# Layer norms of a two-block fp32 transformer kernel: mean read from PSUM, column sums over five tiles of squares, two output blocks on ScalarE

## The reference

```
h = concat(meta, x)
first_block:  even mixer (differential and forgetting attention) -> LN -> squared-ReLU MLP -> LN
              retention -> LN -> squared-ReLU MLP -> LN
second_block: SwiGLU -> LN(ln1); HGRN2 + spatial gating -> LN(ln2);
              cross attention to LN(mem) -> LN(ln3); SwiGLU -> LN(ln4)
LN(x) = (x - mean(x)) * rsqrt(mean((x - mean(x))^2) + 1e-5) * g + b
```

## Time and profile before

| | |
|---|---|
| time, median of 3 runs | 2793.22 us (2792.32 to 2794.8) |
| time of the profiled execution | 2793.86 us |
| span of the profiled execution | 2792.1 us |
| PE busy | 2707.3 us, 97% |
| DVE busy | 1281.0 us, 46% |
| ACT busy | 1016.3 us, 36% |
| POOL busy | 283.2 us, 10% |
| mean granted TensorE clock | 0.987 of full |

### The profile page before, as it was taken

One profiled execution on the slowest core, in us unless ns is written; L12 is line 12 of the kernel. 1 busy time (PEld: TensorE's weight loads), 2 busy tenths in 40 slices (PEclk: granted clock), 3 DMA queues, 4 the chain that ended last, 5 costly groups with the idle time before them and its releaser, 6 DMA issues.

```text
span 2792.1 us, 39535 instructions
## 1 busy us (share of the span) xinstructions
PE 2707.3 (97%) x16362; PEld 2360.0 (85%) x16362; DVE 1281.0 (46%) x2178; ACT 1016.3 (36%) x1630; POOL 283.2 (10%) x357
## 2 busy tenths in 40 slices
PE   8999999999999999999999999999999999999997
PEld 7888899999988888788888888888888887888886
DVE  5544654334532323563334543435657655633333
ACT  4554443222322223352223432323567443522221
POOL 0000300001200000210000310002211121200003
PEclk9999999999999999999999999999999999999998
DMA  3111233222111212232222132222321212232220
GB/s 139 54 47 47 83 123 107 91 91 77 46 61 63 97 61 76 91 106 91 98 98 91 70 118 98 91 84 68 121 76 66 93 46 99 82 101 97 95 64 31
DMA packets 66531, 232.94 MB, mean 83 GB/s; under 512 B 8880, under 2 KB 9264, under 8 KB 65968
## 3 DMA queue, kind: packets, MB, share of 16 engines
q1 hardware_dynamic: 66352, 230.41, 24.8%
HBM read 228.25 MB, written 2.10 MB: 83 GB/s over the span
## 4 chain that ended last, share of the span: by engine, by line
PE 86%; DVE 5%; ACT 4%; POOL 2%; issue 2%; DMA 1%; SPq 0%; DVEq 0%; POOLq 0%; ACTq 0%
PE ps L578 75%; PE ps L887 2%; POOL R L2624 2%; PE ps L1013 1%; PE ps L588 1%; DVE R L1890 1%; PE ps L767 1%; PE ps L727 1%; DVE HT L1884 1%; ACT HT L1240 1%; POOL S L2610 1%; PE ps L874 1%; PE ps L598 1%; PE ps L1110 1%; PE ps L611 1%
## 5 line engine op out<-in xcount | busy, mean ns | idle before, releaser
L578 PE MATMUL ps<-XH,WH 128*128 128x264 f32 (+2 forms) x1856 | 538.3, 332 | 14.4 <-DVE XL L2584 8.6
L578 PE MATMUL ps<-XH,LENT 128*128 128x512 f32 (+2 forms) x2096 | 532.1, 343 | 8.0 <-DVE XL L1906 7.9
L578 PE MATMUL ps<-XL,WH 128*128 128x264 f32 (+2 forms) x1856 | 523.6, 324 | 0.0
L578 PE MATMUL ps<-XH,WL 128*128 128x264 f32 (+2 forms) x1856 | 522.7, 324 | 0.0
L578 PE MATMUL ps<-HH,LENT 128*128 128x264 f32 (+2 forms) x2220 | 491.1, 319 | 1.9 <-DVE LENT L1862 1.9
L1862 DVE TENSOR_TENSOR WL<-RAW,WH 128x1024 fp32r<-128x1024 f32 (+1 forms) x232 | 286.5, 1235 | 270.9 <-ACT WH L1210 270.6
L578 PEld LDWEIGHTS ps<-XH,LENT 128*128 128x128 f32 x2096 | 359.1, 190 | 60.0 <-DVE XL L1906 11.8
L578 PEld LDWEIGHTS ps<-HH,LENT 128*128 128x128 f32 x2220 | 361.4, 190 | 32.0 <-DVE LENT L1862 2.3
L578 PEld LDWEIGHTS ps<-XH,WH 128*128 128x128 f32 x1856 | 319.1, 189 | 56.7 <-issue 19.1
L578 PEld LDWEIGHTS ps<-XH,WL 128*128 128x128 f32 x1856 | 318.9, 189 | 28.1
L578 PEld LDWEIGHTS ps<-XL,WH 128*128 128x128 f32 x1856 | 319.1, 189 | 26.6
(11 more groups left out here) (215 smaller groups left out, 2625.1 us busy)
## 6 DMA issues: line engine op xcount, KB each, us to landing
RAW<-in_wf SPq DMA_DIRECT2D x128, 512.0 KB, 3.3
RAW<-in_wr SPq DMA_DIRECT2D x48, 512.0 KB, 3.3
RAW<-in_wg SPq DMA_DIRECT2D x44, 512.0 KB, 3.3
RAW<-in_wu SPq DMA_DIRECT2D x44, 512.0 KB, 3.3
RAW<-in_wd SPq DMA_DIRECT2D x32, 512.0 KB, 3.3
RAW<-in_we SPq DMA_DIRECT2D x24, 512.0 KB, 3.3
RAW<-in_wm SPq DMA_DIRECT2D x24, 512.0 KB, 3.3
RAW<-in_wro SPq DMA_DIRECT2D x16, 512.0 KB, 3.3
```

Source lines behind the costliest of these rows:

```text
L578: mm = e.matmul(o[:, to:to + m], wt, xt[:, k, c0 + a * m:c0 + (a + 1) * m], start=(n == 0 and j == 0), stop=(n == nk - 1 and j == 2))
```

## The change

- The total is multiplied by a matrix `PART` of 1/1024 instead of `ONE`, so PSUM holds the mean. VectorE subtracts it from there. ScalarE's copy of the mean (L1231) and the signal `mean` are gone; the bank is given back after the last subtraction.
- VectorE adds only square 3 to square 1. `stat` takes five tiles: `HT` slots 2 (squares 1 and 3), 6 (square 5), 1 (squares 0, 2, 4), 3 (square 6), 4 (square 7).
- Blocks 2 and 5 of `r_out` are written by ScalarE (`r_act`), behind the `XH` of the same block, in all norms but `mem`.
- ScalarE's wait for the previous half's `r_out` stays, but now stands before the table load and the squares only.
- At attention's end, 3 of the 7 steps of `ends[1]` stay ahead of `even_back(41)`, 2 stand between its transposes and the value product, 2 behind the value product.
- In the ends of `ln10`, `quiet` is set from the third end on.

```diff
@@ tensor, layer_norm
         def layer_norm(ln, half, T, sums, mark, pump, first):
             pump(first)
-            o = bank(("total", ln, half), 1, (S.mean, ln, half))
+            o = bank(("total", ln, half), 1, (S.centre, ln, half, 7))
             w.wait_ge(*mark)
-            e.matmul(o[:, 0:T], ONE[:, :], sums, start=True, stop=True).then_inc(*S.total(ln, half))
+            w.wait_ge(*S.const["one"])
+            e.matmul(o[:, 0:T], PART[:, :], sums, start=True, stop=True).then_inc(*S.total(ln, half))
             pump(17)
-            rstd((ln, half), [(HT[:, 1, 0:T], S.add_pool[(ln, half, 4)]), (HT[:, 2, 0:T], S.add_dve[(ln, half, 7)])],
+            rstd((ln, half), [(HT[:, 2, 0:T], S.add_dve[(ln, half, 3)]), (HT[:, 6, 0:T], S.sq[(ln, half, 5)]),
+                              (HT[:, 1, 0:T], S.add_pool[(ln, half, 4)]), (HT[:, 3, 0:T], S.sq[(ln, half, 6)]),
+                              (HT[:, 4, 0:T], S.sq[(ln, half, 7)])],
                  T, (S.normed, ln, half, 7), pump, 3)
@@ all three, even_back
             if i == 4:
-                pump(1)
+                pump(1 if t < 7 else 2)
@@ all three, even
             even_back(40, pump)
-            for k in range(7):
-                next(ends[1])
+            pump = pumping(ends[1])
+            pump(3)
             even_back(41, pump)
+            pump(2)
@@ scalar, layer_norm
             w.wait_ge(*S.total[ln, half])
             if normed[0]:
                 w.wait_ge(*S.r_out[normed[0]])
-            e.activation(HT[:, 0, 0:T], acc(("total", ln, half), 1)[:, 0:T], ACT.Copy, scale=inv).then_inc(*S.mean(ln, half))
+                if normed[0][0] != "mem":
+                    w.wait_ge(*S.r_act[(*normed[0][:2], ACT_OUT[-1])])
...
+                if ln != "mem" and k in ACT_OUT:
+                    w.wait_ge(*S.normed[ln, half, k])
+                    e.activation(res(k), HT[:, T_SLOT[k], 0:T], ACT.Identity, bias=pcol(ln + "b", k),
+                                 scale=pcol(ln + "g", k)).then_inc(*S.r_act(ln, half, k))
                 pump(3)
@@ scalar and vector, down_norm
-            for nm, idx in ENDS[ln]:
+            for n, (nm, idx) in enumerate(ENDS[ln]):
+                ah.quiet = ln == "ln10" and n > 1
@@ vector, layer_norm
             pump(first)
+            mean = acc(("total", ln, half), 1)[:, 0:T]
             for k in range(8):
-                w.wait_ge(*S.mean[ln, half])
+                w.wait_ge(*S.total[ln, half])
                 w.wait_ge(*ready(k))
-                e.tensor_tensor(res(k), res(k), HT[:, 0, 0:T], ALU.subtract).then_inc(*S.centre(ln, half, k))
-                if k in (4, 6):
-                    add_square(k - 1)
+                e.tensor_tensor(res(k), res(k), mean, ALU.subtract).then_inc(*S.centre(ln, half, k))
+                if k == 4:
+                    w.wait_ge(*S.sq[ln, half, 3])
+                    e.tensor_tensor(HT[:, 2, 0:T], HT[:, 2, 0:T], HT[:, SQ_SLOT[3], 0:T],
+                                    ALU.add).then_inc(*S.add_dve(ln, half, 3))
                 pump(1)
-            add_square(6)
-            add_square(7)
```

More of the change, by code:

```diff
@@ L286, in build_program @@
     ID = sb("ID", [P, P])
-    ONE = sb("ONE", [P, P])
+    ONE, PART = sb("ONE", [P, P]), sb("PART", [P, P])
     SM = sb("SM", [P, 256])
@@ L525, in first_steps, with out_mark @@
         return (6, 16 if ln == "ln1" else 8)[half]
+    ACT_OUT = (2, 5)
+    def out_mark(ln, half, k):
+        return (S.r_act if ln != "mem" and k in ACT_OUT else S.r_out), (ln, half, k)
     def sums_at(name, idx, half):
@@ L1904, in lower @@
                 w.wait_ge(*S.x_hi[ln, half, k])
-                w.wait_ge(*S.r_out[ln, half, k])
+                sig, event = out_mark(ln, half, k)
+                w.wait_ge(*sig[event])
                 e.tensor_tensor(XL[:, k, c:c + T], res(k), XH[:, k, c:c + T].bitcast(F32),
@@ L1921, in layer_norm @@
                 for k in range(8):
-                    r_mark[k][half] = (S.r_out, (ln, half, k))
+                    r_mark[k][half] = out_mark(ln, half, k)
         def residual(name, idx, m, c, T, half, alpha):
@@ L2622, in layer_norm @@
             for k in range(8):
-                w.wait_ge(*S.normed[ln, half, k])
-                e.tensor_scalar(res(k), HT[:, T_SLOT[k], 0:T], pcol(ln + "g", k), pcol(ln + "b", k), ALU.mult,
-                                ALU.add).then_inc(*S.r_out(ln, half, k))
+                if out_mark(ln, half, k)[0] is S.r_out:
+                    w.wait_ge(*S.normed[ln, half, k])
+                    e.tensor_scalar(res(k), HT[:, T_SLOT[k], 0:T], pcol(ln + "g", k), pcol(ln + "b", k), ALU.mult,
+                                    ALU.add).then_inc(*S.r_out(ln, half, k))
                 for m in between.get(k, ()):
@@ L2646, in down_norm @@
                 layer_norm(ln, half, T // 2, lambda k: R[:, k, c:c + T // 2], dst, {} if half else between)
+        e.memset(PART[:, :], 1.0 / 1024).then_inc(*S.const("part"))
         e.memset(ONE[:, :], 1.0).then_inc(*S.const("one"))
@@ L2756, in sync @@
             for half in (0, 1):
-                w.wait_ge(*S.r_out["ln4", half, k])
+                sig, event = out_mark("ln4", half, k)
+                w.wait_ge(*sig[event])
             e.dma_start(out[:, k, :], R[:, k, NM:TW]).then_inc(*S.out_done(k))
```

10 lines of the change are left out of this document (2 added, 8 removed).

## The result

The changed kernel takes **2802.35 us** (median of 7 runs, 2799.74 to 2808.92) against 2793.22 (7 runs of the kernel before beside it, 2792.32 to 2794.8). The ratio is 1.0032, with a 95% interval of 1.0023 to 1.0042: slower by 9 us. The forecast was 2791.6; its own case ended at 2798 and the widest range named at 2800. The profiled execution is the longest of the seven (2808.92 us, span 2807.1), so its granted clock of 0.984 overstates the loss.

The account below looks back on a forecast made before the run. TensorE, busy 97% of the span, was taken as the bound. Terms +2.4 - 2.4 - 2.0 - 1.0 + 1.4 = -1.6 us gave 2792.3 from the profiled 2793.86, or 2791.6 us as median; range 2786 to 2798.

Parts of the forecast that it names:

- The second part of the norm: Output blocks 2 and 5 on ScalarE: `XL` waits in six first halves fall, -2.0 us, bounds -5 to +3.
- Waits that go at the statistics: TensorE's waits in the norms' statistics go outside ln4's last half, restarts included: 19.8 us removed.
- three leads: Norm statistics: square taken directly, mean's copy gone, two adds fewer; with four tiles' time, over 3 us of lead.
- the slow add: VectorE's add before the statistics in ln4's last half; the first tile was expected ready behind it about 2776.5.
- Work that comes: Three more tiles of one-column matmuls per norm half on TensorE: 22.2 us added, net +2.4 with the waits removed.
- Attention's end: Moved steps cover the waits at value product and eighth steps: -2.4 us, bounds 0 and -2.8.
- `quiet`: In ln10's ends nothing is left to hold back from the third end on; TensorE's 2.91 us wait stays: 0.
- The last half of ln4: At the kernel's end, squares begin earlier and five tiles end near 2780.9: -1.0 us, between 0 and -3.
- The clock: Low-clock stretches behind the norms' statistics: one more of 3.41 us than now, +1.4 us.
- the edge between 2.19 and 2.27 us: Norm halves whose statistics and wait took 2.27 us or more lost clock; those of 2.19 or less did not.
- the clock falls in every half: Rival: eight spared norm halves also fall to the low clock, +11 in place of +1.4, 2801 us; chance 0.13.
- The clock recovers: Rival: seven 256-column norm halves stay at full clock, three of 264 fall, -9.4 us, 2781 us; chance 0.16.

Follow-up runs that it names:

- a_noact: The changed kernel with all eight output blocks written by GpSimd, none by ScalarE; 2792.42 us, ratio 0.9993.
- b_mean: The kernel before with the mean read from PSUM (ScalarE's copy gone) as the only change; 2776.86 us, ratio 0.9938.
- a_two_noact: The changed kernel with two tiles of squares and all output blocks on GpSimd; mean from PSUM and moved attention steps stay; 2776.65 us, ratio 0.9934.
- a_twice: a_two_noact with each statistic's tiles run through a second time, the attention's statistics included; 2806.29 us, ratio 1.0046.
- a_one: The changed kernel with one tile and GpSimd's output blocks, but five tiles and ScalarE's blocks in ln4's second half; 2781.52 us, ratio 0.9957.

## Why the prediction was wrong

**The failed step is "The second part of the norm".** It forecast -2.0 us, with a bound of +3. The step measured +9.9 us in the changed kernel (2802.35 less 2792.42) and +8.4 alone. Without it the terms make +0.4 and 2793.6 us, and a_noact took 2792.42. The words that were wrong are "block 7 is ready 0.3 us earlier": the last `XL` of a first half comes 0.93 us later. The following of the queues took it that GpSimd was the brake and that blocks 2 and 5 would be late on their own; in the trace the lateness stays in VectorE's order and passes on to `normed` and `XH` of later blocks. About half of it is `XL` subtractions that GpSimd's output blocks now slow down (0.68 against 0.43 us), which the step had no term for, and VectorE's late queue also holds up the `WL` of weight panels (7.8 against 3.7 us of waits). The second halves, where the lead panel's relu and square stand behind the output block, were not counted at all; by the `XL` waits (14.0, 18.5, 21.9) they carry nearly half of it, at full clock more, so the share is open. The bound of +3 counted the six first halves alone.

That a_noact comes within 1.2 us of the other terms' 2793.6 is luck: it is the sum of 17.3 us won by the mean, which no term held at that size, and some 16 us lost by the tiles, where the two terms on them made +2.4 with the gain counted in.

**Waits that go at the statistics:** right in size (24.2 to 2.8 us, forecast 19.8 with the restarts), wrong in cause. The argument listed three leads and never asked what one would do alone. The mean from PSUM takes the waits from 24.2 to 10.9 us without any added tile (7.1 and 3.8 in b_mean). It was seen as a copy of 0.38 us; that a subtraction which starts behind a GpSimd addition takes 0.55 us longer was missed, and it is some 10 of the 17 us. The same holds for the adds of squares: "the slow add" of the last half is one.

**Work that comes:** right. L604 is busy 21.2 us longer against 22.2 forecast. (The half of `mem` was left out of the count; 228 matmuls came, not 216.) By the Trainium skill's issue floor (TensorE: Matmul & The Clock Gate, Back-to-back issue gap), about 25 ns each, an estimate for the 216 matmuls is 5.4 us; L604 does not agree, with its 21.2. The sum +2.4 of these two steps hid what mattered: on top of the mean, the tiles are 15.8 us of loss.

**Attention's end:** right, -2.4 forecast, -2.9 measured alone, and both waits are gone. (Its bound of -2.8 should read -2.7, and the 76 idle us at the start are 84.8 by the earlier trace rows; nothing rests on either.) With the mean beside it no gain of it is left that the medians could show (2776.65 against 2776.86).

**`quiet`:** the total in ln10 waits 1.92 us in the changed kernel and 3.27 in a_two_noact, which has the same edit, against 2.91 before; the waits go with what else is late. No run of its own was made. Between b_mean, without the edit, and a_two_noact, with it, the order of instructions is the same on VectorE, ScalarE and GpSimd throughout, and on TensorE but for the steps moved at attention's end, so it is nothing here.

**The last half of ln4:** from its total to the end 18.55 us against 19.37, -0.8 for a forecast of -1.0. But it is the mean again: in b_mean the same stretch takes 18.0 us. The chain after (timelines of PE and ACT), against the earlier trace rows:

```profile
2788.55 1.19 PE L631 MATMUL ps<-S,PART 128*128 128x256 f32 x2 [2.28 <-POOL S L2624]
...
2790.23 1.74 ACT L1251 ACTIVATE HT<-R 128x256 f32<-128x256 f32 x5
...
2792.54 4.40 PE L604 MATMUL ps<-ONE,HT 128*128 128x1 f32 x20 [2.81 <-DVE HT L1904]
...
2797.59 1.19 PE L617 MATMUL ps<-ID,SM 128*128 128x128 f32 x4 [0.64 <-DVE SM L1893]
```

Here the clock is low and twenty matmuls take 4.40 us with nothing beside them.

**The clock:** forecast +1.4 us, measured +4.5 over all runs (38.0 less 33.5), +1.8 in a_noact. The stretches behind statistics lie inside the 25 to 50 us that the text gave: eleven of them, 44 us in the profiled execution, against eight and 37.5. But the edge between 2.19 and 2.27 us that the term rested on is not there. In the changed kernel the statistics take 2.15 us in twelve of the thirteen halves of 256 columns. Behind eight of them the clock fell, though 2.19 us had been spared before, and behind four it did not: the length of the statistics does not decide alone. That the profiled execution has three more such stretches and not one, and all runs together 4.5 us and not 1.4, shows how weak the term was. Of the rivals, "the clock falls in every half" named the right time (2801 us) with the wrong mechanism, at a chance of 0.13; the decisive loss was not among the rivals, but a bound of +3 in a term. "The clock recovers" did not happen.

## What to carry to other kernels

When a change has several parts that attack the same wait, price each alone: the cheapest one may take the whole gain, and the others are then cost. Work moved to a less busy engine is not free when it stands ahead of what the critical engine waits for; follow the in-order queues for first and second halves alike, down to the last block. Before moving work between engines, look at whether VectorE reads two operands from SBUF beside GpSimd, at the longest instructions of a group and not only at its mean. Reading one from PSUM gave about 0.3% here, and 0.6% with the copy gone, by the smallest edit of the change.

## What the hardware showed that I had not expected

The granted clock falls behind one-column matmuls with TensorE never idle. Stretches of the changed kernel (length, PE busy us and matmuls, PEld, DVE, ACT, POOL, granted clock, DMA share, GB/s):

```profile
1191.10:1194.52 3.42, 3.42 (x32) 3.42 (x32) 0.17 (x1) 0.26 (x1) 0.00 (x0) 1.00 0.02 5
1194.52:1197.93 3.41, 3.41 (x18) 3.41 (x18) 2.37 (x6) 1.46 (x3) 1.97 (x3) 0.50 0.00 0
...
1563.17:1566.58 3.41, 3.41 (x32) 3.41 (x32) 0.17 (x1) 0.26 (x1) 0.00 (x0) 1.00 0.00 0
1566.58:1569.99 3.41, 3.41 (x18) 3.41 (x18) 2.32 (x6) 1.40 (x3) 1.97 (x3) 0.50 0.00 0
```

TensorE is busy for 3.41 of 3.41 us before both falls, with the 20 statistics matmuls of 1191.04 and 1563.12 in it, and then runs 18 panel matmuls in a stretch at 1.2 GHz instead of the 30 of the earlier trace rows. Ten falls of the changed kernel have no idle time before them. In a_two_noact, with 8 such matmuls a half of 256 columns, the mean loss to the clock is 25.0 us, with 20 a half (a_noact) 35.3, with 16 and the attention's doubled (a_twice) 40.4. a_one has the fewest and loses 28.3, with more waits. And b_mean, with as many as the kernel before and 13 us less of waits at them, loses 24.4 instead of 34.0. So both one-column matmuls and waits take the clock down; how the two add up is open.

The other surprise is the shared way to SBUF, and that here it was a wait and not a slower rate. A VectorE subtraction of 0.42 us with both operands in SBUF that started behind a GpSimd addition took 0.94 to 1.00 us, until 0.28 to 0.30 us after the addition's end; one that started ahead of it was untouched. No list of waits shows this time, since VectorE counts as busy in it. It stood in 21 of 128 subtractions, and with one operand in PSUM in none.
